# A decoder trunk in exact fp32: the attention scores as three products of rounded parts, and a different first product

## The chip, the cores and the metric

The kernel runs on one NeuronCore of a Trainium2 chip. The metric is the device time of one execution in microseconds (us). Times of a trace are counted from the start of its span. TensorE is the matrix engine (PE in the profile; PEld is its weight load), VectorE is DVE, ScalarE is ACT, GpSimd is POOL, and SyncE (SP) issues most DMAs.

## The reference

x has 256 tokens of 1024 features. Each of two layers is a half-step SwiGLU network, a token mixer, and another half-step SwiGLU network, all behind an RMS norm. The first mixer is sparse attention with three branches over 16 heads of 64 (4 key/value heads), the second is attention with a forget gate over 16 heads. Cut to the lines whose products the change touches:

```python
# NSA layer: compressed, selected and window branch
s_c = jnp.einsum('bqgrd,bngd->bgrqn', qc, k_cmp).astype(jnp.float32) * scale + head_bias(t5_bucket(dist_c))
s_s = jnp.einsum('bqgrd,bgqld->bgrql', qc, k_g).astype(jnp.float32) * scale + bias_s
s_w = jnp.einsum('bqgrd,blgd->bgrql', qc, k_w).astype(jnp.float32) * scale + head_bias(t5_bucket(dist_w))
# FoX layer
s = jnp.einsum('bhqd,bhkd->bhqk', qc, k) * scale + cq[..., None] - cT[:, :, None, :]
```

With 256 tokens all 4 blocks are selected and the window covers everything, so both branches see all earlier keys. The compressed branch has 15 block keys for each of 4 groups.

## The kernel before

**Products.** A product of 512 output columns is made by `three` (L401): the left and the right operand are each split into a rounded part (`hi`, type fp32r, one pass through the array) and the remainder (`lo`), and hi x hi, hi x lo and lo x hi are summed in PSUM. ScalarE casts each weight unit (`hi`, L909; 128x2048) and VectorE subtracts (`lo`, L1298). The scores are not made so: `scores` (L604) and `cmp_scores` (L798) multiply plain fp32 operands `qT`, `kT` and `kcb`. An fp32 product shows as two matmuls with two weight loads, an fp32r product as one of each.

**Order.** The order on each engine is written out by hand; engines meet at semaphores. TensorE's program is L696 to L903: FFN 0, the NSA layer, FFN 1, the shared keys and values, FFN 2, the FoX layer, FFN 3. Weights come in units of 1 MB through three slots.

**Scores.** `scores(n, kidx, p)` makes one head pair's 256x256 causal scores: token tile 1 against 256 keys, then tile 0 against 128 keys, each for two heads. The heads lie on partitions 0 to 63 and 64 to 127. It is called 24 times, 16 in NSA and 8 in FoX, and in the loop `items` it stands between `turn_probs` (transposes of the probabilities) and `values`. VectorE adds the bias and takes the maximum (`add_max`, L1444), ScalarE takes the exponentials (`exps`, L1046).

**Keys and queries.** Keys and queries are turned by TensorE in rounds (`round_`, L584) into the banks `tb[0]` and `tb[1]`. A round waits until both engines have copied the round two before it (`s_ra`, `s_rd`). Of a key round ScalarE copies the lower 64 partitions (`lower`, L1037) and VectorE the upper 64 (`upper`, L1434). Of a query round (`q_half`, L1042 and L1439) ScalarE copies the first 256 columns, then VectorE the other 256.

**Compressed scores.** `cmp_layer2` (L786) makes the compressed keys; VectorE copies them into `kcb`, a layout with zeros (L1610), then makes `vblk` (L1614). `cmp_scores` multiplies 8 head pairs x 2 token tiles of `qT` (128 partitions) with 30 columns of `kcb`. After the fourth pair it waits for rounds 10 and 11 (`rounds_copied(12)`, L803). ScalarE's copies of these rounds come behind `exps(2)`, which waits for `add_max(2)` on VectorE, which comes behind the `kcb` and `vblk` work (L1658 to L1666).

**Start.** TensorE runs `warm_up(10)` (ten transposes of the identity), turns the gains and the first token tile, runs `warm_up(10)` again and enters `first_chunk_of_all` (L432). Its first product waits for `s_half1`: ScalarE casts the first half of unit 0 (two k-tiles, L1079) and VectorE subtracts (L1504). After two k-tiles TensorE turns the second token tile, whose copies run on ScalarE and VectorE (`turned_half`).

Of the kernel before, what the change touches and what calls it, by code (L numbers as in the profile page):

```python
# [101 lines left out]
def yoco_trunk(nc, x, norm_g, ffn_w_in, ffn_w_out, nsa_w_in, nsa_cmp_pos, nsa_cmp_w1, nsa_cmp_w2,  # L102
               nsa_w_out, rel_bias, kv_norm_g, fox_w_kvf, fox_b_f, fox_w_q, fox_w_out, final_g, out):
    ctx = ExitStack()
    with ctx:
# [21 lines left out]
        qT = sb("qT", [P, H // 2, SEQ])  # L127
        nat = sb("nat", [P, 4096])
        kT = sb("kT", [P, 8, SEQ])
# [17 lines left out]
        kcb = sb("kcb", [P, G, 2, NCMP])  # L147
# [19 lines left out]
        kd = nat[:, 0:4096].rearrange("p (t k g u d) -> p t k g u d", t=NT, k=4, g=G, u=2)  # L167
# [26 lines left out]
        gwlo = glo[:, :, :].rearrange("p a n -> p (a n)")  # L194
        onat = xn[:, :, :].rearrange("p t (h d) -> p t h d", h=H)
# [192 lines left out]
        def _(pe):  # L388
# [43 lines left out]
            def first_chunk_of_all(banks):  # L432

                pe.wait_ge(s_half1, 1)
                pe.wait_ge(s_tlo, 1)
                for k in range(2):
                    rows_of(0, 0, 0, k, banks[0][:, :])
# [158 lines left out]
            def kv_round(r, kind, g0):  # L596
                round_(r, [lambda t, g=g: kd[:, t, kind, g].rearrange("p u d -> p (u d)")
                           for g in (g0, g0 + 1)])
# [5 lines left out]
            def scores(n, kidx, p):  # L604
# [3 lines left out]
                for t in (1, 0):  # L608
                    keys = (t + 1) * P
                    c0 = 0 if t else SEQ  # L610
                    for h in range(2):
                        rows = slice(h * DH, (h + 1) * DH)
                        mm = pe.matmul(acc[2 * (n % 2) + h][:, c0:c0 + keys], qT[rows, p, t * P:(t + 1) * P],  # L613
                                       kT[rows, kidx, 0:keys], start=True, stop=True)
# [82 lines left out]
            warm_up(10)  # L697
# [8 lines left out]
            warm_up(10)  # L706
# [200 lines left out]
        def _(act):  # L907
# [171 lines left out]
            act.copy(whi[0][:, 0:UNIT // 2], raw[0][:, 0:UNIT // 2]).then_inc(s_half0, 1)  # L1079
# [25 lines left out]
            def kv_copy(bank, kind, a, used):  # L1105
                act.wait_ge(s_used, used)
                act.mul(kd[:, 0, kind], bank[:, 0:KVD].rearrange("p (g d) -> p g d", d=DH).unsqueeze(2)
# [55 lines left out]
            for r in range(2):  # L1163
                lower(4 + r, kT[0:DH, 2 * r:2 * r + 2, :])
# [730 lines left out]
```

## Time and profile before

| | |
|---|---|
| median of 3 runs | 1065.62 us (1064.27 to 1069.48) |
| the profiled execution | 1069.5 us, its span 1067.5 us |
| TensorE busy | 1048.2 us, 98% of the span |
| VectorE, ScalarE, GpSimd busy | 56%, 49%, 7% |
| the chain that ended last | TensorE 96%, VectorE 2%, ScalarE 1%, issue 1% |
| mean granted TensorE clock | 0.989 |

The chain follows the work that ended last back to its beginning. The starts and lengths of matmuls overlap, since they are pipelined: the time that one takes of its queue is the distance to the next start. A length given to a group of the timeline reaches from the first start to the last end.

### The profile page before, as it was taken

How to read it: one execution, taken by the hardware profiler on the slowest of the kernel's cores; microseconds unless marked ns; L12 is line 12 of the kernel's file. 1: busy time of each engine (PE TensorE's matmuls, PEld its weight loads, DVE VectorE, ACT ScalarE, POOL GpSimd, SP SyncE). 2: the span in 40 equal slices, each digit the busy share in tenths (PEclk: the TensorE clock that was granted, in tenths of full speed). 3: DMA queues.
4: the chain of work that ended last, by engine and by line, in shares of the span. 5: the costliest groups of instructions: out<-in, count | busy, mean ns of one | idle time of the engine just before them, and what ended most of it. 6: DMA issues, size and time to landing. Idle time of an engine off the chain costs nothing.

```text
span 1067.5 us, 14133 instructions
## 1 busy us (share of the span) xinstructions
PE 1048.2 (98%) x5147; PEld 871.8 (82%) x5147; DVE 598.7 (56%) x832; ACT 525.7 (49%) x691; POOL 73.4 (7%) x108
## 2 busy tenths in 40 slices
PE   8999999999999999999999999999998999999997
PEld 7888888888788888888888788888887888888886
DVE  5554454777475564455466775445565556555444
ACT  7444434756475554434455544443465646334444
POOL 0040000000012000000000390000000000000000
PEclk9999999999899999999999999999999999999999
DMA  7776757447301365555545665555544136555541
GB/s 239 236 199 217 213 188 243 158 159 237 118 2 41 109 206 190 185 176 196 193 150 170 236 198 196 196 168 188 195 158 158 41 104 214 189 183 196 196 157 40
DMA packets 128709, 182.45 MB, mean 171 GB/s; under 512 B 5960, under 2 KB 100272, under 8 KB 128544
## 3 DMA queue, kind: packets, MB, share of 16 engines
q1 hardware_dynamic: 127040, 176.18, 49.9%
q0 software_dynamic: 1456, 5.72, 2.3%
q8 instruction: 24, 0.39, 0.2%
q14 instruction: 13, 0.11, 0.0%
q10 hardware_dynamic: 176, 0.05, 0.0%
HBM read 180.34 MB, written 1.59 MB: 170 GB/s over the span
## 4 chain that ended last, share of the span: by engine, by line
PE 96%; DVE 2%; ACT 1%; issue 1%; DMA 0%; ACTq 0%; DVEq 0%
PE inb L403 15%; PE inb L405 15%; PE inb L404 15%; PE acc L403 13%; PE acc L405 13%; PE acc L404 13%; PE inb L640 2%; PE acc L613 2%; PE tb L512 2%; PE tb L625 2%; PE inb L637 1%; PE tb L592 1%; PE acc L397 0%; PE tb L397 0%; DMA rel_s<-in_rel_bias 0%
## 5 line engine op out<-in xcount | busy, mean ns | idle before, releaser
L1320 DVE TENSOR_TENSOR wlo<-raw,whi 128x2048 fp32r<-128x2048 f32 x108 | 250.1, 2316 | 233.4 <-ACT whi L927 233.4
L927 ACT CAST whi<-raw 128x2048 fp32r<-128x2048 f32 x108 | 206.5, 1912 | 216.0 <-PE acc L405 117.8
L403 PE MATMUL inb<-whi,thi 128*128 128x512 f32 x720 | 281.8, 391 | 0.0
L405 PE MATMUL inb<-whi,tlo 128*128 128x512 f32 x720 | 280.6, 390 | 0.0
L404 PE MATMUL inb<-wlo,thi 128*128 128x512 f32 x720 | 280.3, 389 | 0.0
L405 PEld LDWEIGHTS inb<-whi,tlo 128*128 128x128 f32 x720 | 135.2, 188 | 28.5
L404 PEld LDWEIGHTS inb<-wlo,thi 128*128 128x128 f32 x720 | 135.3, 188 | 27.8
L403 PEld LDWEIGHTS inb<-whi,thi 128*128 128x128 f32 x720 | 135.2, 188 | 27.7
L1303 DVE TENSOR_TENSOR wlo<-raw,whi 128x2048 fp32r<-128x2048 f32 x55 | 129.5, 2358 | 46.0 <-ACT whi L914 45.8
L403 PE MATMUL acc<-whi,ghi 128*128 128x512 f32 x320 | 128.6, 402 | 0.0
L405 PE MATMUL acc<-whi,glo 128*128 128x512 f32 x320 | 125.2, 391 | 0.0
L404 PE MATMUL acc<-wlo,ghi 128*128 128x512 f32 x320 | 124.7, 390 | 0.0
L914 ACT CAST whi<-raw 128x2048 fp32r<-128x2048 f32 x55 | 105.3, 1920 | 10.5 <-PE acc L405 9.5
L980 ACT ACTIVATE sa<-inb,rstd 128x256 f32<-128x256 f32 x80 | 34.0, 471 | 139.2 <-PE inb L405 139.2
L403 PE MATMUL acc<-whi,thi 128*128 128x512 f32 x224 | 91.3, 408 | 4.5 <-DVE tlo L1350 3.2
L405 PE MATMUL acc<-whi,tlo 128*128 128x512 f32 x224 | 89.2, 398 | 0.0
L404 PE MATMUL acc<-wlo,thi 128*128 128x512 f32 x224 | 89.1, 398 | 0.0
L405 PEld LDWEIGHTS acc<-whi,glo 128*128 128x128 f32 x320 | 60.1, 188 | 12.9
L1367 DVE SCALAR_TENSOR_TENSOR gg<-inb,rstd,sa 128x256 f32<-128x256 f32 x80 | 35.4, 480 | 62.7 <-ACT sa L980 62.7
L404 PEld LDWEIGHTS acc<-wlo,ghi 128*128 128x128 f32 x320 | 60.3, 188 | 11.0
L403 PEld LDWEIGHTS acc<-whi,ghi 128*128 128x128 f32 x320 | 60.2, 188 | 10.9
L403 PEld LDWEIGHTS acc<-whi,thi 128*128 128x128 f32 x224 | 43.1, 193 | 15.4 <-issue 4.3
(231 smaller groups left out, 989.4 us busy)
## 6 DMA issues: line engine op xcount, KB each, us to landing
raw<-in_ffn_w_in SPq DMA_DIRECT2D x174, 512.0 KB, 4.7
raw<-in_ffn_w_out SPq DMA_DIRECT2D x88, 512.0 KB, 4.0
raw<-in_nsa_w_in SPq DMA_DIRECT2D x20, 512.0 KB, 4.1
raw<-in_fox_w_kvf SPq DMA_DIRECT2D x16, 512.0 KB, 4.6
raw<-in_nsa_cmp_w SPq DMA_DIRECT2D x8, 512.0 KB, 4.4
raw<-in_nsa_w_out SPq DMA_DIRECT2D x8, 512.0 KB, 4.9
raw<-in_fox_w_q SPq DMA_DIRECT2D x8, 512.0 KB, 4.2
raw<-in_fox_w_out SPq DMA_DIRECT2D x8, 512.0 KB, 4.4
```

Of the source, the lines that this page charges most:

```text
L403: pe.matmul(o, lh, rh, start=start, stop=False, skip_group_check=True)
L404: pe.matmul(o, lh, rl, start=False, stop=False, skip_group_check=True)
L405: return pe.matmul(o, ll, rh, start=False, stop=stop, skip_group_check=True)
L512: mm = pe.transpose(tb[0][:, k * SEQ + t * P:k * SEQ + (t + 1) * P], gg[:, t, k * P:(k + 1) * P], ident[:, :])
L613: mm = pe.matmul(acc[2 * (n % 2) + h][:, c0:c0 + keys], qT[rows, p, t * P:(t + 1) * P], kT[rows, kidx, 0:keys], start=True, stop=True)
L625: mm = pe.transpose(tb[h][:, i * P:(i + 1) * P], probs[:, n % 2, c:c + P], ident[:, :])
L914: act.copy(whi[u % RING][:, :], raw[u % RING][:, :]).then_inc(s_hi, 1)
L927: act.copy(whi[u % RING][:, :], raw[u % RING][:, :]).then_inc(s_hi, 1)
L980: act.activation(sa[:, t, :], banks[t][:, 0:FC], ACT.Silu, scale=rstd[:, t:t + 1]).then_inc(s_silu, 1)
L1303: dve.tensor_tensor(wlo[u % RING][:, :], raw[u % RING][:, :], whi[u % RING][:, :].bitcast(F32), ALU.subtract).then_inc(s_lo, 1)
L1320: dve.tensor_tensor(wlo[u % RING][:, :], raw[u % RING][:, :], whi[u % RING][:, :].bitcast(F32), ALU.subtract).then_inc(s_lo, 1)
L1367: dve.scalar_tensor_tensor(out=gg[:, t, :], in0=banks[t][:, FC:2 * FC], scalar=rstd[:, t:t + 1], in1=sa[:, t, :], op0=ALU.mult, op1=ALU.mu ...
```

## The change

The change has two parts. First, `qT`, `kT` and `kcb` become rounded, and their remainders are kept in new buffers (`q_lo` and the idle `ghi`, `glo` for queries; `k_lo`; `kcb_lo`). Scores are then sums of three fp32r products. ScalarE now casts all 128 partitions and 512 columns of a round, and VectorE subtracts after it. `nat` is halved to make room, and its key kinds share two slots. Second, at the start, the casts and subtractions of the first two k-tiles are made one k-tile at a time, the first product waits for one only, and the two `warm_up` groups have 13 and 16 transposes instead of 10 and 10.

```diff
-        qT = sb("qT", [P, H // 2, SEQ])
-        nat = sb("nat", [P, 4096])
-        kT = sb("kT", [P, 8, SEQ])
+        qT = sb("qT", [P, H // 2, SEQ], F32R)
+        q_lo = sb("q_lo", [P, H // 4, SEQ], F32R)
+        nat = sb("nat", [P, 2048])
+        kT = sb("kT", [P, 8, SEQ], F32R)
+        k_lo = sb("k_lo", [P, 8, SEQ], F32R)
...
-        kcb = sb("kcb", [P, G, 2, NCMP])
+        kcb = sb("kcb", [P, G, 2, NCMP], F32R)
+        kcb_lo = sb("kcb_lo", [P, G, 2, NCMP], F32R)
...
+        qlo = [ghi[:, 0, :], ghi[:, 1, :], glo[:, 0, :], glo[:, 1, :]] + [q_lo[:, p, :] for p in range(H // 4)]
+        qlo2 = [ghi[:, :, :], glo[:, :, :], q_lo[:, 0:2, :], q_lo[:, 2:4, :]]
...
             def first_chunk_of_all(banks):
-                pe.wait_ge(s_half1, 1)
                 pe.wait_ge(s_tlo, 1)
                 for k in range(2):
+                    pe.wait_ge(s_half1, k + 1)
                     rows_of(0, 0, 0, k, banks[0][:, :])
...
             def scores(n, kidx, p):
...
-                    for h in range(2):
-                        rows = slice(h * DH, (h + 1) * DH)
-                        mm = pe.matmul(acc[2 * (n % 2) + h][:, c0:c0 + keys], qT[rows, p, t * P:(t + 1) * P],
-                                       kT[rows, kidx, 0:keys], start=True, stop=True)
+                    tok = slice(t * P, (t + 1) * P)
+                    for i, (q, k) in enumerate([(qT[:, p, :], kT), (qT[:, p, :], k_lo), (qlo[p], kT)]):
+                        for h in range(2):
+                            rows = slice(h * DH, (h + 1) * DH)
+                            mm = pe.matmul(acc[2 * (n % 2) + h][:, c0:c0 + keys], q[rows, tok],
+                                           k[rows, kidx, 0:keys], start=i == 0, stop=i == 2)
...
-            warm_up(10)
+            warm_up(13)
...
-            warm_up(10)
+            warm_up(16)
...
             def cmp_scores():
...
-                        mm = pe.matmul(inb[1][:, c0:c0 + 2 * NCMP], qT[:, p, t * P:(t + 1) * P],
-                                       kcb[:, p // 2].rearrange("p u n -> p (u n)"), start=True, stop=True)
+                        k_hi, k_low = [k[:, p // 2].rearrange("p u n -> p (u n)") for k in (kcb, kcb_lo)]
+                        mm = three(inb[1][:, c0:c0 + 2 * NCMP], qT[:, p, tok], qlo[p][:, tok], k_hi, k_low,
+                                   True, True)
...
# ScalarE
-            def lower(r, dst):
+            def key_hi(r, c):
                 act.wait_ge(s_rt, r + 1)
-                act.copy(dst, tb[r % 2][0:DH, :]).then_inc(s_ra, 1)
+                act.copy(kT[:, c:c + 2, :].rearrange("p k n -> p (k n)"), tb[r % 2][:, :]).then_inc(s_ra, 1)
             def q_half(r, i):
-                act.copy(qT[:, 2 * i, :], tb[r % 2][:, 0:SEQ]).then_inc(s_ra, 1)
+                act.copy(qT[:, 2 * i:2 * i + 2, :].rearrange("p k n -> p (k n)"), tb[r % 2][:, :]).then_inc(s_ra, 1)
...
-            act.copy(whi[0][:, 0:UNIT // 2], raw[0][:, 0:UNIT // 2]).then_inc(s_half0, 1)
+            for k in range(2):
+                act.copy(whi[0][:, k * CW:(k + 1) * CW], raw[0][:, k * CW:(k + 1) * CW]).then_inc(s_half0, 1)
...
# VectorE
-            def upper(r, dst):
-                dve.wait_ge(s_rt, r + 1)
-                dve.tensor_copy(dst, tb[r % 2][DH:P, :]).then_inc(s_rd, 1)
+            def key_lo(r, c):
+                dve.wait_ge(s_ra, r + 1)
+                dve.tensor_tensor(k_lo[:, c:c + 2, :].rearrange("p k n -> p (k n)"), tb[r % 2][:, :],
+                                  kT[:, c:c + 2, :].rearrange("p k n -> p (k n)").bitcast(F32),
+                                  ALU.subtract).then_inc(s_rd, 1)
             def q_half(r, i):
-                dve.wait_ge(s_rt, r + 1)
                 dve.wait_ge(s_ra, r + 1)
-                dve.tensor_copy(qT[:, 2 * i + 1, :], tb[r % 2][:, SEQ:2 * SEQ]).then_inc(s_rd, 1)
+                dve.tensor_tensor(qlo2[i].rearrange("p k n -> p (k n)"), tb[r % 2][:, :],
+                                  qT[:, 2 * i:2 * i + 2, :].rearrange("p k n -> p (k n)").bitcast(F32),
+                                  ALU.subtract).then_inc(s_rd, 1)
...
-            dve.wait_ge(s_half0, 1)
-            dve.tensor_tensor(wlo[0][:, 0:UNIT // 2], raw[0][:, 0:UNIT // 2],
-                              whi[0][:, 0:UNIT // 2].bitcast(F32), ALU.subtract).then_inc(s_half1, 1)
+            for k in range(2):
+                dve.wait_ge(s_half0, k + 1)
+                dve.tensor_tensor(wlo[0][:, k * CW:(k + 1) * CW], raw[0][:, k * CW:(k + 1) * CW],
+                                  whi[0][:, k * CW:(k + 1) * CW].bitcast(F32), ALU.subtract).then_inc(s_half1, 1)
...
                 for u in range(2):
-                    dve.tensor_copy(kcb[u * DH:(u + 1) * DH, :, u, :],
-                                    inb[1][u * DH:(u + 1) * DH, 0:GN].rearrange("p (g n) -> p g n", g=G))
+                    rows = slice(u * DH, (u + 1) * DH)
+                    step(dve.tensor_copy(kcb[rows, :, u, :], inb[1][rows, 0:GN].rearrange("p (g n) -> p g n", g=G)))
+                    dve.tensor_tensor(kcb_lo[rows, :, u, :], inb[1][rows, 0:GN].rearrange("p (g n) -> p g n", g=G),
+                                      kcb[rows, :, u, :].bitcast(F32), ALU.subtract)
...
# GpSimd
-            pool.memset(kcb[:, :, :, :], 0.0).then_inc(s_const, 1)
+            pool.memset(kcb[:, :, :, :].bitcast(F32), 0.0)
+            pool.memset(kcb_lo[:, :, :, :].bitcast(F32), 0.0).then_inc(s_const, 1)
```

Key and value copies write `kd[:, t, kind % 2]` instead of `kd[:, t, kind]`; calls of `lower` and `upper` become calls of `key_hi` and `key_lo` at the same places.

## Rows read from the trace of the kernel before

**Rows 1.** The page: busy time and share by engine; shares of the chain by engine.

```profile
PE 1048.2 (98%) x5147; PEld 871.8 (82%) x5147; DVE 598.7 (56%) x832; ACT 525.7 (49%) x691; POOL 73.4 (7%) x108
...
PE 96%; DVE 2%; ACT 1%; issue 1%; DMA 0%; ACTq 0%; DVEq 0%
```

**Rows 2.** Waits of TensorE: who waited for whom, total us, times, longest.

```profile
PE acc L613 <- issue: 2.4, 1, 2.4
PE inb L805 <- DVE qT L1442: 2.1, 1, 2.1
```

**Rows 3.** Timeline of one score call: start, us, engine, line, out<-in, shapes, xcount.

```profile
298.37 0.49 PE L613 MATMUL acc<-kT,qT 64*128 64x256 f32 x2
...
299.01 0.28 PE L613 MATMUL acc<-kT,qT 64*128 64x128 f32 x2
...
298.36 0.19 PEld L613 LDWEIGHTS acc<-kT,qT 64*128 64x128 f32 x2
...
298.90 0.19 PEld L613 LDWEIGHTS acc<-kT,qT 64*128 64x128 f32 x2
```

**Rows 4.** The chain in order of time, one score call each: start, us, what.

```profile
288.27 1.58 PE acc L613 x8
...
298.44 0.85 PE acc L613 x8
```

**Rows 5.** The chain in order of time, 282 to 289 us.

```profile
282.68 1.49 ACT work L1051 x4
...
284.87 0.42 DVE qT L1442
...
285.43 2.84 PE inb L805 x16
```

**Rows 6.** Timeline, 279 to 285 us, VectorE, TensorE and ScalarE.

```profile
279.58 0.45 DVE L1610 COPY kcb<-inb 64x60 f32<-64x60 f32 x2
...
281.39 1.97 PE L805 MATMUL inb<-kcb,qT 128*128 128x30 f32 x16 [0.15 <-DVE low L1614]
...
284.08 0.62 ACT L1044 COPY qT<-tb 128x256 f32<-128x256 f32 x2
```

**Rows 7.** Weight loads grouped by line and form: busy us, mean ns | idle before.

```profile
L404 PEld LDWEIGHTS acc<-wlo,fhi 128*128 128x128 f32 x32 | 6.0, 188 | 1.4
...
L404 PEld LDWEIGHTS acc<-wlo,fhi 128*60 128x60 f32 x32 | 4.2, 132 | 0.1
```

**Rows 8.** Table of stretches: busy by engine, then granted clock, DMA share, GB/s.

```profile
286.30:293.00 6.70, 6.70 (x33) 5.51 (x33) 1.61 (x10) 1.16 (x3) 0.00 (x0) 0.50 0.01 2
...
297.00:334.00 37.00, 36.94 (x300) 31.25 (x300) 30.23 (x146) 28.28 (x74) 9.35 (x9) 1.00 0.01 1
```

**Rows 9.** Copies from PSUM grouped by line and form: busy us, mean ns.

```profile
L989 ACT CAST ghi<-tb 128x512 fp32r<-128x512 f32 x40 | 23.2, 579 | 7.2 <-PE tb L512 7.2
...
L1040 ACT COPY kT<-tb 64x512 f32<-64x512 f32 x8 | 4.2, 579 | 3.7 <-PE tb L592 3.6
...
L1044 ACT COPY qT<-tb 128x256 f32<-128x256 f32 x8 | 2.9, 368 | 5.6 <-PE tb L592 5.5
...
L1376 DVE TENSOR_TENSOR glo<-tb,ghi 128x512 fp32r<-128x512 f32 x40 | 27.3, 683 | 0.1
...
L1437 DVE COPY kT<-tb 64x512 f32<-64x512 f32 x8 | 5.2, 690 | 0.8 <-PE tb L592 0.7
```

**Rows 10.** Timeline of the start, 7 to 14 us.

```profile
7.23 2.39 PE L693 MATMUL acc<-ident 128*128 128x128 f32 x10
...
8.31 1.22 DVE L1504 TENSOR_TENSOR wlo<-raw,whi 128x1024 fp32r<-128x1024 f32 x1
...
9.58 0.79 PE L403 MATMUL acc<-whi,thi 128*128 128x512 f32 x1
...
11.88 0.63 PE L405 MATMUL acc<-whi,tlo 128*128 128x512 f32 x1
...
13.38 1.14 ACT L955 ACTIVATE thi<-acc,gains 128x128 fp32r<-128x128 f32 x4 [3.32 <-PE acc L397]
```

More of the change, by code:

```diff
@@ L165, in yoco_trunk @@
         rel_s = sb("rel_s", [NB, H])
-        kd = nat[:, 0:4096].rearrange("p (t k g u d) -> p t k g u d", t=NT, k=4, g=G, u=2)
+        kd = nat[:, :].rearrange("p (t k g u d) -> p t k g u d", t=NT, k=2, g=G, u=2)
         vd = vx[:, 0:NT * 4 * VP].rearrange("p (t a i n) -> p t a i n", t=NT, a=2, i=2)
@@ L596, in kv_round @@
             def kv_round(r, kind, g0):
-                round_(r, [lambda t, g=g: kd[:, t, kind, g].rearrange("p u d -> p (u d)")
+                round_(r, [lambda t, g=g: kd[:, t, kind % 2, g].rearrange("p u d -> p (u d)")
                            for g in (g0, g0 + 1)])
@@ L804, in cmp_scores @@
                         c0 = t * H * NCMP + 2 * p * NCMP
-                        mm = pe.matmul(inb[1][:, c0:c0 + 2 * NCMP], qT[:, p, t * P:(t + 1) * P],
-                                       kcb[:, p // 2].rearrange("p u n -> p (u n)"), start=True, stop=True)
+                        tok = slice(t * P, (t + 1) * P)
+                        k_hi, k_low = [k[:, p // 2].rearrange("p u n -> p (u n)") for k in (kcb, kcb_lo)]
+                        mm = three(inb[1][:, c0:c0 + 2 * NCMP], qT[:, p, tok], qlo[p][:, tok], k_hi, k_low,
+                                   True, True)
                 mm.then_inc(s_sc, 1)
@@ L1106, in kv_copy @@
                 act.wait_ge(s_used, used)
-                act.mul(kd[:, 0, kind], bank[:, 0:KVD].rearrange("p (g d) -> p g d", d=DH).unsqueeze(2)
+                act.mul(kd[:, 0, kind % 2], bank[:, 0:KVD].rearrange("p (g d) -> p g d", d=DH).unsqueeze(2)
                         .broadcast_to([P, G, 2, DH]), rstd[:, 0:1])
@@ L1163, in _ @@
             for r in range(2):
-                lower(4 + r, kT[0:DH, 2 * r:2 * r + 2, :])
+                key_hi(4 + r, 2 * r)
             hi(U_NSA + 7)
@@ L1168, in _ @@
             for r in range(2):
-                lower(6 + r, kT[0:DH, 4 + 2 * r:6 + 2 * r, :])
+                key_hi(6 + r, 4 + 2 * r)
             hi(U_NSA + 9)
@@ L1228, in _ @@
             for i in range(2):
-                lower(12 + i, kT[0:DH, 2 * i:2 * i + 2, :])
+                key_hi(12 + i, 2 * i)
             hi(U_KV + 6)
             for i in range(2, 4):
-                lower(12 + i, kT[0:DH, 2 * i:2 * i + 2, :])
+                key_hi(12 + i, 2 * i)
             hi(U_KV + 7)
@@ L1534, in kv_copy @@
                 dve.wait_ge(s_used, used)
-                dve.tensor_scalar(kd[:, 1, kind], bank[:, 0:KVD].rearrange("p (g d) -> p g d", d=DH)
+                dve.tensor_scalar(kd[:, 1, kind % 2], bank[:, 0:KVD].rearrange("p (g d) -> p g d", d=DH)
                                   .unsqueeze(2).broadcast_to([P, G, 2, DH]), rstd[:, 1:2], None, ALU.mult)
@@ L1586, in _ @@
             for r in range(2):
-                upper(4 + r, kT[DH:P, 2 * r:2 * r + 2, :])
+                key_lo(4 + r, 2 * r)
             windows(1)
@@ L1592, in _ @@
             for r in range(2):
-                upper(6 + r, kT[DH:P, 4 + 2 * r:6 + 2 * r, :])
+                key_lo(6 + r, 4 + 2 * r)
             lo(U_NSA + 9)
@@ L1706, in _ @@
             for i in range(2):
-                upper(12 + i, kT[DH:P, 2 * i:2 * i + 2, :])
+                key_lo(12 + i, 2 * i)
             step(dve.tensor_scalar(fcor, fcor, -1.0, None, ALU.add))
@@ L1718, in _ @@
             for i in range(2, 4):
-                upper(12 + i, kT[DH:P, 2 * i:2 * i + 2, :])
+                key_lo(12 + i, 2 * i)
             lo(U_KV + 7)
```

## The prediction

> **What bounds the kernel now.** I read the page first: TensorE is busy 98% of the span and the chain that ended last runs over it for 96% [rows 1]. So a change is worth what it does to TensorE's own queue, plus what it does to the few places where TensorE waits. The chain's shares by line size the prize: the attention scores (L613) hold 2% of the span, about 19 us, the compressed scores (L805) some 5 us. Everything else that the change edits is copies on ScalarE and VectorE, and they count only where TensorE waits for them. The list of waits has two such places: 2.1 us for the last query copy of the NSA layer, and 2.4 us at the start of the FoX scores [rows 2]. The start of the kernel is the third.
>
> **The score product, 24 calls.** One call is four fp32 products: two heads on different halves of the rows, with 256 and then 128 moving columns. Each product is two matmuls, so there are eight. The reader should look at the start times in one call [rows 3]: the matmuls start two at a time (four pairs, from 298.37 to 299.01), and so do the weight loads (four pairs, from 298.36 to 298.90). The two heads work side by side, each with a queue of its own. In such a queue one fp32 matmul of 256 columns takes 0.21 us, one of 128 columns 0.11. In front lies 0.11 us for the first load and behind 0.10 us before the next full-array load starts. That is 0.11 + 0.21 + 0.21 + 0.11 + 0.11 + 0.10 = 0.85 us, which the chain shows [rows 4].
>
> After the change a head has six matmuls of one pass instead of four of two. Moving its columns costs 3 x 0.107 + 3 x 0.053 = 0.48 us instead of 0.64. But a weight load comes with each matmul, and it costs about 0.11 us whatever moves. Fp32 matmuls that move 30 columns come as slowly as 0.112 us each: 16 from 281.39 take 1.97 us, of which 0.27 is the length of the last one, so 15 steps fill 1.70 [rows 6]. For the rounded type I take the load from the group means of the load engine: 60 weight columns take 132 ns and 128 take 188, a slope of 0.83 ns a column, so 128 columns are 0.107 us plus a latency that overlaps [rows 7]. So six matmuls come 0.112 us apart: 0.11 + 5 x 0.112 + 0.053 + 0.10 = 0.82 us instead of 0.855, a gain of 0.035. At half clock (four of the calls, 1.58 us [rows 4]) loads double too, and the gain is the shorter last product, 0.11. Sum: 20 x 0.035 + 4 x 0.11 = **-1.1 us**. The bounds: -4.5 us if loads hide completely (0.16 a call, 0.32 when slow), and the two bad cases below.
>
> **The compressed scores.** 16 products of 30 columns become 48 matmuls instead of 32. No row tiling here, so 0.112 us each, 0.213 at half clock (286.3 to 293.0 was at 0.50 of 2.4 GHz [rows 8]). The first 8 of the 16 extra ones (0.9 us) lie ahead of the wait in which TensorE is idle 2.1 us [rows 2], and cost nothing; without that cover they would cost 0.9. The second half runs behind the wait: 16 matmuls took 2.84 us there, because the clock fell partway [rows 5].
>
> **The wait before the second half ends later.** It ends on the last query copy. In time: VectorE's two kcb copies from 279.58, vblk, add_max; ScalarE's four exponentials from 282.68 (1.49) and its two query copies from 284.08; VectorE's second query copy, 284.87 to 285.29 [rows 5, 6]. Two things lengthen it. (1) kcb_lo: each of two copies is now followed by a wait for itself and a subtraction; with 0.22 us a copy [rows 6] and about 0.04 us for the wait, that is +0.5 us, all on VectorE ahead of add_max, on which the exponentials wait. (2) ScalarE now copies 512 columns (0.58, the price of L989, instead of 0.37) and VectorE subtracts 512 (0.68, as L1376, instead of 0.42) [rows 5, 9]. First copy ends 284.66, subtractions 284.74 to 286.03 instead of an end at 285.29: +0.75. TensorE resumes at 286.65 instead of 285.43. Its idle time stays near 2.0 us, as the first half now lasts longer. I assume that the clock falls as it did, so 24 matmuls at 0.213 follow: 286.65 + 5.1 = 291.8, instead of 288.27: **+3.5 us**. This is the largest term and the least certain: with no fall, 24 x 0.112 ends at 289.3 (+1.1, and the items behind, 4.8 us at half clock, give back 2.4: -1.3); with half clock for half as long again as the 6.7 us of [rows 8], +1.7 more: +5.2. I take the middle, since the same idle time produced the fall.
>
> **Other copies.** Keys: ScalarE's cast costs what the 64-row copy did (0.58 each), VectorE's subtraction what its copy did (0.68 against 0.69) [rows 9]. VectorE now starts after ScalarE, half a microsecond later at one round; the next unit's remainder is needed over 3 us later: 0. If that cover were gone: 0.6. Queries, first pair of FoX: 0.21 on ScalarE and 0.1 in VectorE's start-to-end step ahead of scores(16), and the 2.4 us wait behind hangs on the same chain through add_max: **+0.3**. The other query rounds have cover, 0.1 at worst. The halved `nat` buffer adds no wait: its kinds 0 and 1 are turned before kinds 2 and 3 are written. GpSimd's second memset: 0.2 us of an idle engine, ahead of its DMA issues, which wait for units used.
>
> **The start.** The first product starts at 9.58, when L1504 is done; the six products up to 11.88 stand 0.46 us apart, which for 512 columns is the level of 1.2 GHz [rows 10]. Ahead of it stand two groups of ten small transposes, ten in 2.4 us, so 0.22 us each, with a pause of 0.5 us near 4.04 that waits for the gains' data. The change fills the pause (3 x 0.22 = 0.66, ending at 4.48 when the data is there at 4.53: no delay) and puts 16 in the second group. What follows is ScalarE's copy at 13.38, which waits for TensorE's second set of transposes [rows 10]; it carries the head start or the loss through, since the later loads and casts have 2 to 3 us to spare. If the clock rises no earlier: 7.23 + 16 x 0.22 = 10.7, six products, second transposes 0.5 us later: +0.5. If it is up before 7.2: the 16 take 1.8 us and end at 9.0, when the first k-tile's remainder is ready (8.31 [rows 10] + 0.68), and ScalarE's copy starts near 11.0: -2.4. Between these I take **-1.0**.
> The Trainium skill (TensorE: Matmul & The Clock Gate, PE-mode transpose) says that transposes do not count as busy in the way products do. By that rule the extra ones raise nothing and the term is +0.5. The trace leans that way: 8 us of near-continuous transposes left the first products at the lower level.
>
> **Sum.** -1.1 + 3.5 + 0.3 - 1.0 = +1.7 us. The profiled execution took 1069.5 us (span 1067.5, 2.0 around it) and becomes 1071.2; it was the longest of three, the median is 1065.6, so the forecast for the median is **1067 us**. One part in 200, 5.3 us, is about what a measurement of this kernel can tell from no change. The forecast's own range is 1062 to 1071: the start's ends (-1.4, +1.5), the stall's ends (-4.8, +1.7), not all together.
>
> **Rivals.**
> *Passes rule, not loads (faster).* If loads of the rounded type hide behind other work, a score call loses a quarter of its 0.64 us of moving: -4.5 us in all; the stall gives only +1 since fewer slow matmuls are load-bound; the start gives -2.4: -6 us, **1059.5**. Against it: the slope of the load times [rows 7] and the 0.112 us spacing [rows 6]; for it: no row shows a rounded 128-column load exposed. The Trainium skill (FP8 and Floating Point Precision, TensorE Precision Notes) counts true fp32 as four passes through the array, and three one-pass products would then cost three quarters; that is this result.
> *Short moving operands (slower).* Every rounded matmul of the trace moves 256 or 512 columns; none moves 128. If the rounded type moves fewer than 256 columns at the fp32 rate, a 128-column product takes 0.21 instead of 0.11 us: three a call, +0.3 (0.6 slow), 20 x 0.3 + 4 x 0.6 = +8.4: **1075.5**. The compressed scores would not change (4 x 30 columns is less than a load). It decides as soon as a 128-column rounded matmul takes over 0.15 us.
> *Loads of the two halves in turn.* If the rounded loads do not run in pairs as fp32's do [rows 3], 12 x 0.107 + 0.2 = 1.5 us a call instead of 0.85: +16: **1083**. Only if the pairing is fp32's alone.
> *The item loop loses its clock.* It ran 37 us at 1.00, 2.4 GHz [rows 8]; products that wait for loads leave the array emptier. Half of that stretch at half clock: +18: **1085**.
>
> **How the numbers follow.** Forecast 0.59; passes rule 0.12; short operands 0.15; loads in turn 0.05; clock lost 0.04; 0.05 for none of them. The range 1059.5 to 1075.5 holds forecast, passes rule and short operands, 0.86 with their edges, some 0.8 counting their own spread. Faster by over 0.5% (below 1060.3): 0.12. Slower by over 0.5% (above 1070.9): 0.15 + 0.05 + 0.04, and 0.02 of the forecast: 0.26. Within: 0.62.
>
> **What the changed profile would show.** Right: a score call of 0.82 us on the chain, matmul pairs 0.11 us apart; 48 compressed matmuls, 0.112 apart, the wait before the 25th ending near 286.7 after a kcb chain longer by 0.5; ScalarE's first copy of the second token tile near 12.4 or earlier. Wrong: a call at 0.70 (passes), at 1.1 (short operands, gaps of 0.21 at 128 columns), at 1.5 (loads single), or items at half clock in the table of stretches.

## The result and the profile after

The changed kernel takes **1069.01 us** (median; 1067.0 to 1083.92), the kernel before 1066.93 us (1063.84 to 1069.48), each timed 20 times. The ratio is 1.0032, 95% interval 1.0016 to 1.0048. So the change costs 2.1 us by the medians and 3.4 us by the ratio, within the 0.5% that I called no change; the forecast was 1067 us with a chance of 0.62 for "within". Most executions lie between 1067 and 1071 us, but three of the 20 took 1081 to 1084; a ratio leaves out executions more than 1.5% above their kernel's fastest, the quoted ranges keep them (and two single executions of about 1757 us, one each of two experiments, at a mean clock of 0.55 to 0.56). The profiled execution took 1070.6 us, its span 1068.6.

The page of the changed kernel looks as before [rows 1]:

```profile
PE 1050.2 (98%) x5268; PEld 877.4 (82%) x5268; DVE 598.8 (56%) x835; ACT 527.4 (49%) x692; POOL 73.5 (7%) x109
...
PE 97%; DVE 1%; ACT 1%; issue 0%; POOL 0%; DVEq 0%; POOLq 0%
```

The waits of TensorE in the changed kernel (who waited for whom, total us, times, longest) answer to [rows 2]; L408 is now the compressed score product, L620 the attention scores:

```profile
PE acc L620 <- issue: 2.4, 1, 2.4
PE inb L408 <- DVE q_lo L1453: 1.9, 1, 1.9
...
PE acc L620 <- ACT qT L1053: 1.0, 1, 1.0
...
PE inb L408 <- DVE low L1630: 0.6, 1, 0.6
```

Both old waits are still there at their old size, and the one on `qT` ahead of the first FoX score call grew from 0.6 us to 1.0. The last line is a wait ahead of the first half of the compressed scores, 0.62 us long in the timeline; before it was 0.15 us [rows 6]. The timeline of one score call of the changed kernel answers to [rows 3]. Read the starts: six pairs, 0.11 to 0.12 us apart but for the first and the fourth, whose successors start 0.23 and 0.06 us after them:

```profile
298.73 0.39 PE L620 MATMUL acc<-kT,qT 64*128 64x256 f32 x2
298.96 0.28 PE L620 MATMUL acc<-k_lo,qT 64*128 64x256 f32 x2
299.07 0.28 PE L620 MATMUL acc<-kT,q_lo 64*128 64x256 f32 x2
299.19 0.22 PE L620 MATMUL acc<-kT,qT 64*128 64x128 f32 x2
299.25 0.27 PE L620 MATMUL acc<-k_lo,qT 64*128 64x128 f32 x2
299.36 0.27 PE L620 MATMUL acc<-kT,q_lo 64*128 64x128 f32 x2
```

The chain of the changed kernel in order of time, around the compressed scores and two score calls (start, us, what), answers to [rows 4, 5]:

```profile
278.95 0.23 DVE kcb L1625
279.20 0.21 DVE kcb_lo L1626
279.43 0.23 DVE kcb L1625
...
282.55 1.49 ACT work L1060 x4
284.04 0.48 ACT qT L1053
284.54 1.30 DVE q_lo L1453 x2
285.98 0.36 PE inb L408
...
291.25 1.47 PE acc L620 x9
...
301.73 0.84 PE acc L620 x12
```

TensorE resumes at 285.98 (before 285.43), although it had entered the layer 0.56 us earlier, and reaches the next score call at 291.25 (before 288.27).

The granted clock in the tables of stretches, first of the kernel before, then of the changed kernel (stretch in us, its length, busy by engine as PE, PEld, DVE, ACT, POOL, then the clock, DMA share, GB/s):

```profile
286.25:293.07 6.82, 6.82 (x33) 5.63 (x34) 1.68 (x10) 1.23 (x3) 0.00 (x0) 0.50 0.01 2
337.45:340.86 3.41, 3.41 (x10) 2.63 (x9) 0.00 (x0) 0.00 (x0) 0.00 (x0) 0.50 0.47 151
822.14:828.97 6.83, 6.83 (x37) 5.86 (x33) 2.82 (x13) 2.23 (x6) 0.00 (x0) 0.50 0.47 151
846.03:849.45 3.42, 3.40 (x8) 2.75 (x9) 0.00 (x0) 0.00 (x0) 0.00 (x0) 0.50 0.61 208
```

```profile
284.13:297.78 13.65, 11.80 (x65) 11.23 (x65) 4.73 (x15) 3.93 (x10) 0.00 (x0) 0.50 0.00 0
337.45:340.86 3.41, 1.72 (x13) 1.53 (x13) 1.37 (x4) 1.33 (x4) 1.29 (x2) 1.00 0.64 181
823.44:830.26 6.82, 6.82 (x42) 6.24 (x39) 3.36 (x13) 2.67 (x6) 0.00 (x0) 0.50 0.46 149
847.33:850.74 3.41, 3.41 (x9) 2.67 (x9) 0.00 (x0) 0.00 (x0) 0.00 (x0) 0.50 0.57 196
```

The stretch at 1.2 GHz around the compressed scores is twice as long as before and begins in the wait itself.

**Where the time went.** I take the first matmul of the hidden activations' turn in each FFN as a mark, and compare the two spans (1067.52 and 1068.60 us):

| stage | before | after | difference |
|---|---|---|---|
| start to FFN 0's turn | 29.71 | 29.22 | -0.49 |
| from there to FFN 1's turn (holds NSA) | 354.40 | 356.41 | +2.01 |
| to FFN 2's turn | 238.84 | 238.09 | -0.75 |
| to FFN 3's turn (holds FoX) | 269.90 | 270.21 | +0.31 |
| to the end | 174.67 | 174.67 | 0.00 |

They sum to +1.08. The -0.75 is one 0.7-us wait of TensorE for the shared keys' weight remainder (VectorE, near 609 us), which the changed kernel's execution doesn't have; no line of the change touches it.

### The profile page after: what moved, and what is told of

Same layout as the page of the kernel before. It is cut to its first block, busy times and chain, and to the rows that moved or that the text cites. A ratio compares the mean times of both kernels' runs of the same rounds, so it can differ in the third digit from the quotient of the medians.

```text
span 1068.6 us, 14372 instructions
## 1 busy us (share of the span) xinstructions
PE 1050.2 (98%) x5268; PEld 877.4 (82%) x5268; DVE 598.8 (56%) x835; ACT 527.4 (49%) x692; POOL 73.5 (7%) x109
## 4 chain that ended last, share of the span: by engine, by line
PE 97%; DVE 1%; ACT 1%; issue 0%; POOL 0%; DVEq 0%; POOLq 0%
PE inb L408 15%; PE inb L410 15%; PE inb L409 15%; PE acc L408 13%; PE acc L410 13%; PE acc L409 13%; PE inb L647 2%; PE acc L620 2%; PE tb L632 2%; PE tb L517 2%; PE inb L644 1%; PE tb L597 1%; PE tb L402 1%; PE acc L700 1%; PE acc L402 1%
## 5 line engine op out<-in xcount | busy, mean ns | idle before, releaser
L408 PE MATMUL inb<-whi,thi 128*128 128x512 f32 x720 | 281.7, 391 | 0.0
L410 PE MATMUL inb<-whi,tlo 128*128 128x512 f32 x720 | 280.5, 390 | 0.0
L410 PEld LDWEIGHTS inb<-whi,tlo 128*128 128x128 f32 x720 | 135.1, 188 | 28.5
L408 PEld LDWEIGHTS inb<-whi,thi 128*128 128x128 f32 x720 | 135.2, 188 | 27.8
L408 PE MATMUL acc<-whi,ghi 128*128 128x512 f32 x320 | 128.5, 402 | 0.0
L410 PE MATMUL acc<-whi,glo 128*128 128x512 f32 x320 | 125.1, 391 | 0.0
L408 PE MATMUL acc<-whi,thi 128*128 128x512 f32 x224 | 90.2, 403 | 3.8 <-DVE tlo L1360 3.2
L410 PE MATMUL acc<-whi,tlo 128*128 128x512 f32 x224 | 88.2, 394 | 0.0
L410 PEld LDWEIGHTS acc<-whi,glo 128*128 128x128 f32 x320 | 60.0, 188 | 12.9
L409 PEld LDWEIGHTS acc<-wlo,ghi 128*128 128x128 f32 x320 | 60.3, 188 | 11.1
L408 PEld LDWEIGHTS acc<-whi,ghi 128*128 128x128 f32 x320 | 60.2, 188 | 10.9
L408 PEld LDWEIGHTS acc<-whi,thi 128*128 128x128 f32 x224 | 42.6, 190 | 14.1 <-issue 3.6
```

Of the source, the lines that this page charges most:

```text
L408: pe.matmul(o, lh, rh, start=start, stop=False, skip_group_check=True)
L409: pe.matmul(o, lh, rl, start=False, stop=False, skip_group_check=True)
L410: return pe.matmul(o, ll, rh, start=False, stop=stop, skip_group_check=True)
```

## Experiments

My theory: weight loads set the pace of the rounded score products, so these save almost nothing; what costs is the NSA wait and the half-clock stretch behind it. The rivals: products of 128 columns are slow in themselves; the start pays for nothing; the clock of the item loop. Each ratio is to the kernel before, timed on the same chip in the same session; its median was between 1066.93 and 1067.53 us each time. `fill`, `reorder`, `narrow` and `start_fill` were timed on another chip than the rest; the kernel before has 1067.11 us there.

### The change in its two parts

`start_only` is the kernel before with the change's start; `scores_only` the changed kernel with the start of before.

```diff
+                    pe.wait_ge(s_half1, k + 1)
...
-            warm_up(10)
+            warm_up(13)
...
-            warm_up(10)
+            warm_up(16)
...
```

> The kernel before with the start of the change alone (13 and 16 warm-up transposes, first product waits for one k-tile). Theory A (the change costs time where TensorE waits for the query copies of the NSA layer, and the start gives a little back): 0.5 us faster than before, as the traces' 0.49 us at the first turn of the hidden layer; the NSA stall unchanged, a wait of 2.1 us before the second half of the compressed scores. Rival B (the start is what costs, by delaying the first product to 10.55 us): 1 to 3 us slower than before.

Measured: 1066.25 us, ratio 0.9999 (0.9987 to 1.0011), against a median of 1067.18 beside it: no change that can be told. Rival B is out.

> The changed kernel with the old start (10 and 10 transposes, first product waits for two k-tiles). Theory A: 2.5 us slower than before (the 2.1 us of the medians plus the 0.5 us that the start gave), a score call at 0.84 us, the compressed scores ending 3 to 4 us later after the same beginning. Rival B: no slower than before. Rival C (the scores themselves are cheaper and something else lost it): score calls under 0.8 us.

Measured: 1069.17 us, ratio 1.0022 (1.001 to 1.0034); beside that the execution at 1758 us. Its profile repeats the changed kernel's stall: it resumes at 285.06, only 0.37 us ahead of the kernel before, though its mark in FFN 0 stands 1.47 us ahead (28.24 against 29.71), so its wait ends 1.10 us later by its own time. The 13.66 us at 0.50 (282.77 to 296.43) begin ahead of the wait here, during the last three matmuls of the first compressed half. So the scores carry the loss, and the start's gain is not to be seen in a median here; its price is taken up further down, where less scatters.

### More and fewer columns for the same loads

`wide`: token tile 0 also moves 256 key columns (the masked ones too).

```diff
-                    keys = (t + 1) * P
+                    keys = SEQ
```

> The changed kernel, where the products of token tile 0 move 256 key columns instead of 128 (the extra scores are written to PSUM and read by nobody; nothing is left out). Theory A (each matmul costs its weight load, about 0.112 us, whatever it moves): a call goes from 0.84 to about 0.90 us (the last matmul moves 0.053 us longer, the rest is hidden), 1.5 us over 24 calls. Rival (moved columns set the time): 3 x 0.053 = 0.16 us more a call, 3.8 us and more over 24 calls. Rival (a rounded matmul is slow below 256 columns): the call gets shorter.

Measured: 1070.68 us (1068.41 to 1073.48), ratio 1.0039 (1.0024 to 1.0053). A call in the chain of `wide`:

```profile
300.47 0.91 PE acc L620 x12
```

and its first five pairs in the timeline:

```profile
300.40 0.39 PE L620 MATMUL acc<-kT,qT 64*128 64x256 f32 x2
300.62 0.28 PE L620 MATMUL acc<-k_lo,qT 64*128 64x256 f32 x2
300.74 0.28 PE L620 MATMUL acc<-kT,q_lo 64*128 64x256 f32 x2
300.85 0.28 PE L620 MATMUL acc<-kT,qT 64*128 64x256 f32 x2
300.98 0.28 PE L620 MATMUL acc<-k_lo,qT 64*128 64x256 f32 x2
```

A third more columns cost 0.91 - 0.84 = 0.07 us a call. All of it lies in the step after the fourth pair, 0.13 us instead of 0.06; the other steps stay as they were. That is theory A's size, 1.7 us over 24 calls, and the medians are 1.7 us apart.

`narrow`: both token tiles move 128 key columns only.

```diff
-                    keys = (t + 1) * P
+                    keys = P
```

> The changed kernel, where the products of token tile 1 move 128 key columns instead of 256; the scores of token tile 1 against keys 128 to 255 are left out, their places in PSUM hold old numbers. Theory A (a weight load per matmul sets the time): a call stays near 0.82 us though a third of its columns is gone. Rival (columns set it): 3 x 0.053 = 0.16 us less, 0.68 us. A second question: the change had 3 of 20 executions of 1081 to 1084 us at a mean clock of 0.973 to 0.975, the kernel before none of 55, the wide variant none of 10. If that comes from an emptier array in the item loop, here at least 3 in 8 executions lie above 1075 us and the table of stretches shows 0.50 within 300 to 335 us.

Measured: 1117.0 us (1114.57 to 1118.84, four executions), ratio 1.0454 (1.0434 to 1.0475). Less work, and 4.5% slower. The table of stretches of `narrow`, over the item loops of NSA and FoX:

```profile
282.14:377.72 95.58, 92.43 (x458) 81.95 (x458) 39.03 (x176) 38.08 (x92) 10.87 (x10) 0.50 0.04 12
859.00:899.96 40.96, 39.47 (x197) 36.22 (x197) 16.71 (x74) 18.70 (x44) 0.00 (x0) 0.50 0.15 48
```

A call here takes 1.47 us at half clock, just what it takes in the changed kernel, which moves half as many columns again: at that clock the time of a call goes by its loads. But TensorE stays at 1.2 GHz for 95.6 and 41.0 us, with work in its queue 96 to 97% of that time. The changed kernel's two stretches in these loops hold 20.5 us; half of the 116.1 us more is 58, and the span is 48.3 us longer (1116.9 against 1068.6), so some of that time was slack or is repaid by the missing columns.

### What the 16 extra compressed matmuls cost

`cmp32` multiplies the rounded compressed operands once in fp32 (32 matmuls, remainders left out).

```diff
-                        mm = three(inb[1][:, c0:c0 + 2 * NCMP], qT[:, p, tok], qlo[p][:, tok], k_hi, k_low,
-                                   True, True)
+                        mm = pe.matmul(inb[1][:, c0:c0 + 2 * NCMP], qT[:, p, tok].bitcast(F32), k_hi.bitcast(F32),
+                                       start=True, stop=True)
```

> The changed kernel, with the compressed scores as one fp32 product of the rounded parts (the remainders q_lo and kcb_lo are made but not multiplied, so the compressed scores lose their low part): 32 matmuls there instead of 48, all copies as in the change. Theory A: 8 fewer matmuls at 0.213 us behind the wait, 1.7 us, and up to one stretch of 3.4 us less at half clock, 1.7 us more: 1.7 to 3.4 us faster than the change. Rival (matmul count doesn't matter, the later copies do): as the change.

Measured: 1068.14 us (1065.32 to 1080.95), ratio 1.0044 (1.0012 to 1.0075). The second half takes 3.59 us instead of 5.27 (285.98 to 291.25), 1.7 less, but in the profile TensorE idles longer ahead of it (2.7 us instead of 1.9), and the stretch at 0.50 lasts 17.07 us (282.55 to 299.62). Three of ten executions took 1074 to 1081 us. The median is 0.9 us below the changed kernel's, the ratio to the kernel before is no smaller: among times so scattered no gain can be told, and theory A's 1.7 to 3.4 us are not shown. In the profile the eight matmuls saved ahead of the wait only make it longer, and the 1.7 us saved behind it are given back by clock: 3.4 us more at 0.50 there, and another stretch of 3.41 us from 340.57, which the changed kernel's execution doesn't have.

### Filling the wait in the changed kernel

`fill` puts 16 transposes of the identity into the wait ahead of the second compressed half; `reorder` puts score call 3 there instead.

```diff
+                        pe.wait_ge(s_nmax, 2)
+                        for _ in range(16):
+                            pe.transpose(acc[2][:, 0:P], ident[:, :], ident[:, :])
```

> The changed kernel, where TensorE makes 16 transposes of the identity (1.75 us) in the wait between the two halves of the compressed scores. Nothing is left out. Theory A (the idle array there lets the granted clock fall to 1.2 GHz, and that, not the waiting, is most of the 2.1 us): the stretch at 0.50 after the wait is gone or starts later; the second half takes 24 x 0.112 = 2.7 us instead of 5.1, two score calls and their neighbours run at full clock: 3 to 6 us faster than the change, 2 to 4 us faster than the kernel before. Rival (the clock falls because matmuls of 30 columns leave the array empty, whatever stands in the wait): the stretch at 0.50 stays, within 1 us of the change.

Measured: 1077.16 us (1068.5 to 1084.15), ratio 1.0074 (1.0038 to 1.011).

```diff
-                    if i + 2 < count:
+                    if i + 2 < count and (n0, i) != (0, 1):
...
+                        scores(3, nsa_keys(3), 3)
```

> The changed kernel, with the score call of item 3 moved into that wait (it needs no query of the two rounds that are waited for). Nothing is left out. Theory A: the call's 0.84 us moves into idle time, -0.84 us where the clock is full and -1.5 us where it would have run at half clock; the wait shrinks from 1.9 to about 1.1 us. If the clock holds, as with the fill, up to 5 us faster than the change. Rival: item 3's call was hidden elsewhere and the loop waits instead, no change.

Measured: 1080.93 us (1065.82 to 1757.39), ratio 1.0047 (1.0014 to 1.008). In either, 6 of 12 executions took 1080 to 1084 us, against 3 of 20 of the changed kernel; the expected gains did not come. The profiled execution of `fill` is one of those; its timeline of TensorE:

```profile
281.19 0.29 PE L409 MATMUL inb<-kcb_lo,qT 128*128 128x30 f32 x1
281.32 0.37 PE L410 MATMUL inb<-kcb,glo 128*128 128x30 f32 x1
281.53 0.37 PE L408 MATMUL inb<-kcb,qT 128*128 128x30 f32 x1
...
283.45 3.67 PE L811 MATMUL acc<-ident 128*128 128x128 f32 x16
```

and the table of the stretch that begins there:

```profile
281.28:325.66 44.38, 44.38 (x236) 41.10 (x237) 18.02 (x81) 17.64 (x44) 0.11 (x1) 0.50 0.00 1
```

The clock falls at 281.28 in the middle of the first compressed half, ahead of the wait and of the filler: the starts, 0.11 us apart until then, are 0.21 apart from 281.32 on. TensorE is busy for all of the next 44.38 us, and stays at 1.2 GHz. `reorder` shows the same from 281.74 to 322.70. The wait of 2 us is therefore not the only thing that takes the clock from the changed kernel. At half clock the 16 transposes take 3.67 us, more than the wait that they fill: the second half starts 20.13 us after the layer's first scores, in the changed kernel 17.78. Filling the wait did not help, and more executions were slow.

### Filling the waits in the fp32 version

`start_fill` is the kernel before with the change's start and the 16 transposes, its scores in fp32; beside `start_only` it adds:

```diff
+                        pe.wait_ge(s_nmax, 2)
+                        for _ in range(16):
+                            pe.transpose(acc[2][:, 0:P], ident[:, :], ident[:, :])
```

> The kernel before (fp32 scores) with the new start and with 16 transposes in the same wait. Nothing is left out. Theory A: the 6.8 us at 0.50 after the wait are gone, 3 us faster than the kernel before, faster than the change by 5 us. Rival: the stretch at 0.50 stays, 0 to 1 us faster than before.

Measured: 1064.84 us (1062.82 to 1066.51), ratio 0.9971 (0.9956 to 0.9986). That is theory A's 3 us. No stretch at 0.50 is left around the compressed scores; three are left elsewhere (335.04 to 338.45, 819.73 to 826.55, 843.62 to 847.03), and `start_fill_all` fills the waits ahead of these:

```diff
+                 pe.wait_ge(s_nmax, 23 if first else 15)
+                 for _ in range(12 if first else 14):
+                     pe.transpose(acc[0][:, 0:P], ident[:, :], ident[:, :])
...
+            pe.wait_ge(s_nmax, 17)
+            for _ in range(20):
+                pe.transpose(acc[0][:, 0:P], ident[:, :], ident[:, :])
```

> The kernel before with the new start and the 16 identity transposes in the NSA wait (as start_fill), and with 20 more ahead of the FoX scores and 14 and 12 ahead of the projections' second halves, where TensorE idles before the other half-clock stretches (335.04 to 338.45, 819.73 to 826.55 and 843.62 to 847.03 us in start_fill, at 0.50). Theory 1, an idle wait of TensorE is what lets its clock fall in each of these places: the three stretches go, which hold 3.4, 6.8 and 3.4 us, half of that lost, 6.8 us together at most; less the transposes that outlast the wait, near 1059 to 1061 us. Theory 2, the stretches have to do with what TensorE does besides waiting (short or load-bound products): at most one of them goes, 1063 to 1066 us as start_fill (1064.84).

Measured: **1059.03 us** (1058.8 to 1060.81), ratio **0.9929** (0.9916 to 0.9943): faster than both kernels. The table of stretches of `start_fill_all` over the four places:

```profile
281.80:294.50 12.70, 11.43 (x99) 10.20 (x99) 7.43 (x35) 6.60 (x18) 0.00 (x0) 1.00 0.01 1
333.00:341.00 8.00, 7.29 (x52) 6.28 (x50) 2.57 (x8) 1.57 (x4) 1.28 (x2) 1.00 0.39 130
814.00:826.00 12.00, 10.58 (x94) 9.45 (x94) 8.46 (x35) 6.16 (x18) 0.00 (x0) 1.00 0.30 89
840.00:849.00 9.00, 8.55 (x56) 7.40 (x55) 1.90 (x5) 1.45 (x3) 0.57 (x1) 1.00 0.17 54
```

and its chain at the first of them:

```profile
285.18 1.94 PE inb L811 x16
287.12 0.85 PE acc L613 x8
```

All four are at 1.00, the second half of the compressed scores takes 1.94 us (before 2.84 [rows 5]), and the next call starts 1.15 us earlier than in [rows 4]. The time is theory 1's.

`fill_all_old_start` differs from it only in the start:

```diff
-                    pe.wait_ge(s_half1, k + 1)
...
-            warm_up(13)
+            warm_up(10)
...
-            warm_up(16)
+            warm_up(10)
...
```

> The kernel before with the transposes in the waits (16, 20, 14 and 12 of them, as start_fill_all) and with its own start. It prices the start part of the change where no stretch at 0.50 behind the start is left to scatter the times (start_fill_all: 1058.8 to 1060.8). If the start part is worth what its term said, 1.0 us, this one takes 1060.0 us; if it is worth the 2.4 us of its lower end, 1061.4; if nothing, as start_only's ratio 0.9999 says, 1059.0. Rival to all of them: the transposes in the waits hold the clock only in company with a clock that rises early at the start; then a stretch at 0.50 is back and it takes 1062 or more.

Measured: 1060.09 us (1059.22 to 1061.85), ratio 0.9945 (0.993 to 0.996). That prices the start part at 1.06 us, or at 1.7 if each is taken against the kernel before of its own session. There are six executions each, whose ranges overlap, and three of the six took 1059.2 us, as long as the kernel with the new start: the size is rough.

### Filling all waits in the rounded version

Both kernels are the changed kernel with the lines of `fill` and `start_fill_all`; `wide_fill_all` has that of `wide` as well:

```diff
-                    keys = (t + 1) * P
+                    keys = SEQ
```

> The changed kernel with both score matmuls moving 256 key columns (as wide), and with the same transposes in the waits. If the rare executions at 1081 to 1084 us come from calls that move few columns for their weight loads, none is seen here, as none was in wide and in the kernel before; 1062 to 1070 us. Theory 1 (the filler keeps the clock once the calls move 1536 columns a head again): no stretch at 0.50 after the NSA wait, and 3 to 5 us less than wide (1070.68). Rival (the clock falls in the compressed scores themselves, as it did in fill at 281.28 us, before the filler): a stretch at 0.50 from 281 to 285 us on, and 1068 to 1071 us.

Measured: 1067.17 us (1064.93 to 1073.51), ratio 1.0009 (0.9991 to 1.0028).

> The changed kernel as it is (token tile 0 moves 128 key columns) with the same transposes in the waits. It differs from wide_fill_all in the columns that token tile 0's score products move, and in nothing else. Theory (the scores' few moved columns per weight load let the clock stay down in the item loop): some of the executions near 1080 us, as in the changed kernel, fill and reorder, with mean clocks near 0.975; the others at 1063 to 1067 (wide_fill_all 1067.17 less 1.6 for 24 shorter calls). Rival (the transposes in all the waits are enough): no execution above 1075, median near 1065.

Measured: 1069.01 us (1065.12 to 1091.64), ratio 1.0024 (0.9997 to 1.0052), 3 of 12 executions above 1080. The profiled executions took 1070.49 and 1071.05 us. The table of stretches of `wide_fill_all`, then of `after_fill_all`:

```profile
281.29:294.94 13.65, 13.65 (x70) 13.06 (x71) 1.73 (x4) 2.65 (x7) 0.00 (x0) 0.50 0.00 1
```

```profile
281.21:288.04 6.83, 6.83 (x35) 6.83 (x34) 1.81 (x4) 2.29 (x6) 0.00 (x0) 0.50 0.01 1
...
827.35:841.00 13.65, 13.65 (x80) 12.85 (x77) 6.79 (x34) 8.18 (x21) 0.00 (x0) 0.50 0.00 0
```

In these two executions the rival of `wide_fill_all` is borne out: with the wait filled, the clock still falls during the first compressed half, which now is 24 matmuls of 30 columns instead of 16. The times say more. `wide_fill_all` is 3.5 us below `wide` (1070.68), as theory 1 had it: 7 of its 12 executions took 1065 to 1067 us at mean clocks of 0.995 to 0.996, where `wide` has 0.986 to 0.991; the other five took 1070 to 1074. Of `after_fill_all`, 6 of 12 took 1065 to 1067, at 0.993 to 0.994. So the filler, which keeps all six executions of `start_fill_all` at 0.997 to 0.999, helps in about half of those here, and no profile of one of these was taken. How the columns bear on the slowest executions shows in the counts above 1075 us, the line that two of the expectations drew:

| kernels | executions | above 1075 us |
|---|---|---|
| rounded, tile 0 moves 128 columns (changed kernel, `scores_only`, `cmp32`, `fill`, `reorder`, `after_fill_all`) | 78 | 20, and 2 near 1757 |
| rounded, 256 columns (`wide`, `wide_fill_all`) | 22 | 0 |
| fp32 scores (`start_only`, `start_fill`, `start_fill_all`, `fill_all_old_start`) | 31 | 0 |
| `narrow` | 4 | 4 |

The first row is uneven: 3 of 20, 0 of 12, 2 of 10, 6 of 12, 6 of 12 and 3 of 12.

## Why the prediction was right, and where it wasn't

**The number.** The terms summed to +1.7 us, and the medians of 20 executions each are 2.1 apart. The forecast stood on a median of three, 1065.6; on 1066.93 it would have been 1068.6, against 1069.01.

**The score call.** Predicted 0.82 us, measured 0.84; at half clock 1.47, as 1.58 - 0.11 said. The reasoning held in the main: three of the five steps are a load's 0.11 to 0.12 us, and `wide` and `narrow` show it from both sides. The 0.23 and the 0.06 us of the other two the sum did not have; the whole call came out only 0.02 us longer. The gain is about 20 x 0.015 + 4 x 0.11 = 0.7 us instead of 1.1. The passes rule, which promised -4.5, is refuted, and so are slow short operands (`wide`) and loads in turn (pairs in the timeline).

**The compressed scores.** Right: 48 matmuls, 0.11 us apart, 0.213 at half clock. The cover for the first eight was there: the wait kept its size, 1.9 us against 2.1. What the prediction did not see is that the work for `kcb_lo` also delays the first half (the wait of 0.62 us instead of 0.15); that lies ahead of the longer wait and is covered by it too.

**The wait.** Predicted: it ends 1.22 us later, at 286.65. Measured 285.98, with the layer's first scores 0.56 us ahead of before (268.20 against 268.76), so 1.11 later by the layer's own time. Its two causes stand in the chain: `kcb_lo` (two subtractions, which with their waits put 0.5 us ahead of `low`, as predicted) and the wider copies (0.48 and 1.30 us). The copies were mis-sized a little: 0.52 us each on ScalarE (283.95, two in 1.04) and 0.65 on VectorE, where the sum had 0.58 and 0.68. No run takes either cause away by itself.

**The stall.** Predicted +3.5 for the end of the second half. Measured 291.25 - 288.27 + 0.56 = 3.54: 1.11 from the wait, 2.43 from the second half (5.27 against 2.84). That is the term I called least certain.

**What I left out.** I let the half-clock stretch keep its end. It lasted 13.65 us instead of 6.82, and the items behind the stall ran 6.5 us at half clock instead of 4.8: +0.9. Against it, the stretch of 3.41 us at 337.45 was not repeated in this execution: -1.7. Together with the calls (-0.5 of the 0.7): 3.54 + 0.9 - 1.7 - 0.5 = 2.2, and the table of stages has 2.01. That the two cancel was luck.

**FoX.** Predicted +0.3; the wait grew by 0.4 and the stage by 0.31.

**The start.** Predicted -1.0, between +0.5 and -2.4. The profile has -0.49, the medians with the other waits filled 1.06. Neither is firm. The mark in FFN 0 lies between 27.26 and 29.53 us in the eleven traces with the new start, and at 28.02, 28.24 and 29.71 in the three with the old one: it moves with the time at which the clock rises, by more than the term. `start_only` has the lower end of my range nearly as I wrote it (first product at 8.93, ScalarE's copy at 11.04). In the profile of the changed kernel the mechanism differed from the middle that I took: the first product came later (10.55 instead of 9.58 [rows 10]) but at full clock two matmuls in. The timeline of the changed kernel (L408 to L410 are the first six products, L964 the copy that was at 13.38 [rows 10]):

```profile
7.22 3.67 PE L700 MATMUL acc<-ident 128*128 128x128 f32 x16
...
10.55 0.72 PE L408 MATMUL acc<-whi,thi 128*128 128x512 f32 x1
...
11.10 0.39 PE L409 MATMUL acc<-wlo,thi 128*128 128x512 f32 x1
...
12.89 0.88 ACT L964 ACTIVATE thi<-acc,gains 128x128 fp32r<-128x128 f32 x3 [2.50 <-PE acc L402]
```

I had asked for 12.4 or earlier and got 12.89, half a microsecond before the old one.

**The item loop's clock.** I gave it 0.04 and 18 us. In the median it did not happen, but it is real: 3 of 20 executions lost 12 to 15 us, with mean clocks of 0.973 to 0.975 against 0.987 to 0.991, and with fewer columns (`narrow`) all four lost. The price was close, the chance too low. The rival's condition ("products that wait for loads leave the array emptier") fits `narrow` and the table of counts, but is not shown to be the cause. Why the fp32 calls, whose matmuls are as busy by the profile, are spared isn't shown either.

**Where the clock falls.** The prediction hung the fall on the wait ("the same idle time produced the fall"). In the kernel before it comes 0.8 us after the wait (286.25), in the changed kernel's profile and in `cmp32` within it (284.13 and 282.55). In the seven other traces with rounded scores it falls earlier, while the first compressed half runs: `scores_only` 282.77, `wide` 282.47, `narrow` 282.14, `reorder` 281.74, `fill` 281.28, `wide_fill_all` 281.29, `after_fill_all` 281.21. In none of the five traces with fp32 scores does it fall there. Three things are new ahead of that point: 24 compressed matmuls instead of 16, rounded score calls, and the wait of about 0.6 us (0.59 to 0.65 in all nine, 0.15 in all five). `cmp32` has 16, and its clock falls 2.8 us after their start, against 4.9 in the kernel before; otherwise no run separates the three.

**Still open.** The fastest executions of the filled rounded kernels took 1065 us, those of the filled fp32 kernel 1059. The stall's matmuls and copies explain 2 to 3 of these 6 us (+1.1 for the wait, 8 more matmuls behind it at 0.11 or 0.21, FoX +0.3, less 0.4 for the calls). The mean clocks, 0.994 to 0.996 against 0.998 to 0.999, are worth another 2 to 5 by estimate (0.002 to 0.005 of 1064 us). I have no profile of such an execution, and leave it there.

## What to carry to other kernels

Before splitting a product into more, cheaper ones, count its weight loads: here, with 128 weight columns and at most 256 moving ones, the load set most of the pace, and three one-pass products gained 0.015 us a call on two-matmul fp32 ones, while their remainders cost copies on a chain that TensorE waits for. Look up the granted clock of every stretch behind a wait; here 62 throw-away transposes in four short waits gave 6.8 us (1060.09 against 1066.93, the start left as it was), where the rewrite of the scores gave nothing. In the kernel with the rewrite the same transposes helped in only half of the executions: look for what the clock did ahead of the wait before filling it. Time such a kernel often enough to see its rare slow group: a change can leave the median and lose 13 us in one execution of seven.

## What the runs showed of the hardware

- **Transposes can bring the clock up, and hold it.** In the profile of `start_only` the 16 transposes ahead of the first product run at full rate, with nothing but small transposes before them: 1.96 us for 16, against 3.67 in the changed kernel's execution above.

```profile
2.76 1.88 PE L693 MATMUL acc<-ident 128*128 128x128 f32 x8
...
4.79 1.09 PE L397 MATMUL tb<-ident,xs 128*128 128x128 f32 x8
...
7.21 1.96 PE L693 MATMUL acc<-ident 128*128 128x128 f32 x16
...
8.93 0.47 PE L403 MATMUL acc<-whi,thi 128*128 128x512 f32 x1
```

  The Trainium skill (TensorE: Matmul & The Clock Gate, PE-mode transpose) says that transposes don't count as busy as products do. These rows and the 1.00 of `start_fill_all` speak against it, and the measurement decides. Not every execution shows it: the clock rose at 4.5 us in this one, but at 11.1 and 13.2 in those of the changed kernel and the kernel before, after their first products (10.55 and 9.58).
- **A TensorE that is busy without a gap can stay at 1.2 GHz**: 44.38 us in `fill` (281.28 to 325.66), with matmuls behind one another all the time.
- **The clock can fall while matmuls run back to back**: in seven traces it fell during the 24 that move 30 columns each, 1.4 to 2.5 us after the first of them (281.21 to 282.77 us). A wait of about 0.6 us ends where they begin; whether it has a share isn't shown.
